# FFN products of 512 columns: the high and the low operand side by side, the RMS factor outside, modulation tiles in other places

## The reference

```python
a = rms_norm(h, norm_ffn[i])
h = h + swiglu(a, ffn_w_gate[i], ffn_w_up[i], ffn_w_down[i])   # (silu(a @ w_gate) * (a @ w_up)) @ w_down, hidden width 2816
```

```python
mod = (jax.nn.silu(c) @ ada_w[i] + ada_b[i])[:, None, :]
mod_c = jax.nn.silu(c_ctx) @ ada_w[i] + ada_b[i]
sh1, sc1, g1, sh2, sc2, g2 = jnp.split(mod, 6, axis=-1)
```

## Time and profile before

| | |
|---|---|
| median of three runs | 2372.78 us (2371.78 to 2374.68) |
| the profiled execution's own time | 2376.23 us |
| its span, first to last instruction | 2374.4 us |
| PE busy | 2285.0 us, 96% |
| VectorE busy | 1706.2 us, 72% |
| ScalarE busy | 1092.3 us, 46% |
| granted TensorE clock, mean | 0.983 |

### The profile page before, as it was taken

How to read it: one execution, slowest core, us unless ns; L and a number is a source line. 1 busy time by engine, 2 the same in 40 slices (tenths; PEclk the granted TensorE clock), 3 DMA queues, 4 the chain that set the end, 5 groups by cost and what they waited for, 6 DMA issues and landing times.

```text
span 2374.4 us, 41274 instructions
## 1 busy us (share of the span) xinstructions
PE 2285.0 (96%) x16984; PEld 2123.7 (89%) x16984; DVE 1706.2 (72%) x3331; ACT 1092.3 (46%) x1968; POOL 0.2 (0%) x4
## 2 busy tenths in 40 slices
PE   7999999999999999999999998999999999998998
PEld 7869999899999999996999986788888888968997
DVE  6678875678777887677787666566877875367667
ACT  4485444564443544447644533544222234275343
POOL 0000000000000000000000000000000000000000
PEclk9899999999999999998999999999999999999999
DMA  6315765347665566641466532022554522423553
GB/s 225 133 46 194 248 210 193 132 154 250 219 203 178 191 242 220 202 173 37 169 242 225 172 107 89 1 72 98 186 166 162 169 89 94 138 81 122 181 180 123
DMA packets 71098, 374.84 MB, mean 158 GB/s; under 512 B 7424, under 2 KB 17664, under 8 KB 38912
## 3 DMA queue, kind: packets, MB, share of 16 engines
q1 hardware_dynamic: 61456, 361.52, 44.6%
q10 hardware_dynamic: 9456, 10.68, 1.5%
HBM read 369.03 MB, written 1.05 MB: 156 GB/s over the span
## 4 chain that ended last, share of the span: by engine, by line
PE 79%; DVE 13%; ACT 4%; DMA 2%; issue 2%; ACTq 0%; DVEq 0%
PE ps L440 74%; DVE w_lo L1558 5%; DMA w_raw<-weights 2%; PE ps L734 2%; ACT w_hi L1042 2%; PE ps L717 2%; DVE ps L1592 1%; DVE hid_f L1927 1%; PE ps L674 1%; DVE a_lo L1558 1%; DVE hid_f L1949 1%; ACT a_hi L1065 1%; PE ps L664 1%; DVE p_ring L2205 0%; DMA X<-x_t 0%
## 5 line engine op out<-in xcount | busy, mean ns | idle before, releaser
L440 PE MATMUL ps<-a_hi,w_hi 128*128 128x256 f32 (+1 forms) x3184 | 941.4, 296 | 39.7 <-DVE w_lo L1558 21.2
L440 PE MATMUL ps<-a_lo,w_hi 128*128 128x256 f32 (+1 forms) x3184 | 932.9, 293 | 0.0
L440 PE MATMUL ps<-a_hi,w_lo 128*128 128x256 f32 (+1 forms) x3184 | 932.6, 293 | 0.0
L1042 ACT CAST w_hi<-w_raw 128x1024 fp32r<-128x1024 f32 (+1 forms) x632 | 593.0, 987 | 499.8 <-DMA w_raw<-weights 498.8
L1558 DVE TENSOR_TENSOR w_lo<-w_raw,w_hi 128x1024 fp32r<-128x1024 f32 (+1 forms) x632 | 699.5, 1148 | 139.6 <-ACT w_hi L1042 139.4
L440 PEld LDWEIGHTS ps<-a_hi,w_hi 128*128 128x128 f32 x3184 | 612.8, 192 | 59.1 <-issue 34.5
L440 PEld LDWEIGHTS ps<-a_lo,w_hi 128*128 128x128 f32 x3184 | 613.0, 193 | 10.7 <-issue 0.2
L440 PEld LDWEIGHTS ps<-a_hi,w_lo 128*128 128x128 f32 x3184 | 612.9, 192 | 10.7
L440 PE MATMUL ps<-hid_hi,w_hi 128*128 128x256 f32 (+1 forms) x1396 | 431.3, 309 | 7.1 <-DVE w_lo L1558 3.1
L440 PE MATMUL ps<-hid_lo,w_hi 128*128 128x256 f32 (+1 forms) x1396 | 427.8, 306 | 0.0
L440 PE MATMUL ps<-hid_hi,w_lo 128*128 128x256 f32 (+1 forms) x1396 | 427.7, 306 | 0.0
(11 more groups left out here) (209 smaller groups left out, 2108.9 us busy)
## 6 DMA issues: line engine op xcount, KB each, us to landing
w_raw<-weights SPq DMA_DIRECT2D x250, 1024.0 KB, 4.8
pe_sb<-weights SPq DMA_DIRECT2D x96, 512.0 KB, 5.6
w_raw<-weights SPq DMA_DIRECT2D x64, 704.0 KB, 4.0
pe_sb<-na_bias ACTq DMA_DIRECT2D x32, 128.0 KB, 2.1
qk<-qk ACTq DMA_DIRECT2D x8, 256.0 KB, 6.9
X<-x_t SPq DMA_DIRECT2D x1, 1024.0 KB, 7.6
X<-c_rows ACTq DMA_DIRECT2D x2, 512.0 KB, 4.5
qk<-ctx_t ACTq DMA_DIRECT2D x1, 1024.0 KB, 5.7
```

The lines of the kernel that those rows point to most:

```text
L440: return nc.tensor.matmul(out, stationary, moving, start=start, stop=stop)
L1042: nc.scalar.copy(w_hi[:, u % SLOTS, c], raw(u, c)).then_inc(hi_split, 1)
```

## The change

Five things are changed together.

1. The high and low operands lie in one tensor (`a_both`, `hid_both`), and in the ffn `wide_tile` makes W_hi [x_hi | x_lo] as one matmul of 512 columns, and adds W_lo x_hi as one of 256 columns into the upper half. The two halves of a PSUM bank are added on the way out: ScalarE copies the upper half (gate and up together, 2 x 256 columns) to SBUF, VectorE adds it to the lower half.
2. The ffn's operand is the unnormalized activation throughout. The gate sum is multiplied with `r_row` before Silu, the up sum isn't, and the output tile of the down part is multiplied with `r_row` before it is added to X. `normalized` goes.
3. Gate and up take the bank pairs (0, 1) and (2, 3) in turn; the first down tile takes bank 0.
4. The order of the splits in gate/up is written out by halves.
5. An ffn has 11 modulation tiles (behind gate/up units 2, 5, 8, ... 20 and behind the down tiles 0, 2, 4, 6); moba gets 4, conv 2, the second nsa 2, the first mlp keeps 36, the last mlp gets 8, with the wait and the sum that finish them.

```diff
-ADA_GATE = [j for j in range(LAZY + 1, FT) if j % 3 != 0]
-ADA_DOWN = range(3)
-ADA_EARLY = 4 * (len(ADA_GATE) + len(ADA_DOWN))
-ADA_MLP = [0, 0, 0, 1, 2, 2, 2, 2] + [1, 1, 1, 1, 2, 2, 2, 2] * 2 + [1, 1, 1] + [0] * 5
+ADA_GATE = range(2, FT, 3)
+ADA_DOWN = range(0, KD, 2)
+ADA_AT = {"ffn": [*ADA_GATE] + [FT + 2 * k + 1 for k in ADA_DOWN], "moba": (1, 3, 5, 7), "conv": (8, 10), "nsa": (0, 2)}
+ADA_EARLY = 4 * len(ADA_AT["ffn"]) + len(ADA_AT["moba"]) + len(ADA_AT["conv"]) + len(ADA_AT["nsa"])
+ADA_MLP = [[0, 0, 0, 1, 2, 2, 2, 2] + [1, 1, 1, 1, 2, 2, 2, 2] * 2 + [1, 1, 1] + [0] * 5,
+           [0, 0, 0, 0, 1, 1, 1, 1] * 2 + [0] * 16]
...
+            def wide_tile(out, high, low, xh, both, start, stop):
+                if not stop:
+                    mm(out, high, both, start, False)
+                last = mm(out[:, S:2 * S], low, xh, False, False)
+                if stop:
+                    last = mm(out, high, both, start, True)
+                return last
...
             def run_ffn(i):                                    # PE
                 operands()
-                a = parts(a_hi, a_lo, CTX)
-                fm_unit("AD", a, between=norm_at)
-                pairs("AD", a, LAZY - 1)
-                operands()
-                pairs("AD", parts(a_hi, a_lo), FT - LAZY)
+                a = wide_parts(CTX)
+                before = cnt.n["D"]
+                wait(pe, taken["A"], cnt.n["A"])
+                for j in range(FT):
+                    if j == 1:
+                        pe.wait_ge(taken["D"], before)
+                    if j >= 2:
+                        pe.wait_ge(taken["A"], cnt.n["A"] - 1)
+                    gate_up(j, a)
...
                 def gate_up(j):                                # ScalarE
+                    gate_sum, at = gate_up_slot[j % 2][:, 0], slice(made[0][0], made[1][0] + 1)
+                    for _, _, (s_, count) in made:
+                        wait(act, s_, count)
+                    wait(act, taken["A"], made[0][1])
+                    nc.scalar.copy(low_slot, ps[:, at, S:2 * S]).then_inc(low_copied, 1)
+                    split_half(u + 2, 0)
+                    act.wait_ge(gate_scaled, h + 1)
+                    nc.scalar.activation(gate_sum, gate_sum, ACT.Silu).then_inc(silu_done, 1)
+                    split_half(u + 2, 1)
                     wait(act, taken["D"], made[1][1] + 1)
                     nc.scalar.copy(hid_hi[:, (h - h0) * S:(h - h0 + 1) * S], t_ring[:, h % 2, 0:S]).then_inc(hid_h, 1)
...
-                def down():                                    # ScalarE
+                def down(k):
                     skip("")
-                    u, [made] = next_unit("D")
+                    u, [made] = unit(cnt, "D", down_banks(k))
+                    bank, p, (s_, count) = made
+                    wait(act, s_, count)
+                    nc.scalar.copy(down_low, ps[:, bank, S:2 * S]).then_inc(low_copied, 1)
                     residual_tile(made, made[1] - d0, gain)
...
                 def gate_up(j):                                # VectorE
+                    both, y = gate_up_slot[j % 2], t_ring[:, h % 2, 0:S]
+                    low_part()                                 # waits for low_copied
+                    v.tensor_tensor(both, ps[:, made[0][0]:made[1][0] + 1, 0:S], low_slot, ALU.add).then_inc(taken["A"], 1)
+                    dve.wait_ge(taken["A"], made[0][1] + 1)
+                    v.tensor_tensor(both[:, 0], both[:, 0], r_row[:, :], ALU.mult).then_inc(gate_scaled, 1)
+                    split_half(u + 2, 0)
+                    dve.wait_ge(silu_done, h + 1)
+                    wait(dve, hid_ready, h - 1)
+                    v.tensor_tensor(y, both[:, 0], both[:, 1], ALU.mult).then_inc(taken["D"], 1)
+                    split_half(u + 2, 1)
                     c = slice((h - h0) * S, (h - h0 + 1) * S)
+                    dve.wait_ge(hid_h, h + 1)
                     minus(hid_lo[:, c], y, hid_hi[:, c]).then_inc(hid_ready, 1)
...
                 def down(k):                                   # VectorE
                     u0, _ = next_unit("")
                     ahead(u0)
-                    u1, [made] = next_unit("D")
+                    u1, [made] = unit(cnt, "D", down_banks(k))
                     bank = ready(made)
-                    x = X[:, k, LAT]
-                    v.tensor_tensor(x, ps[:, bank, 0:S], x, ALU.add).then_inc(taken["D"], 1)
+                    x, total = X[:, k, LAT], down_slot[k % 2]
+                    low_part()
+                    step(v.tensor_tensor(total, ps[:, bank, 0:S], down_low, ALU.add))
+                    sync()
+                    step(v.tensor_tensor(total, total, r_row[:, :], ALU.mult))
+                    sync()
+                    v.tensor_tensor(x, x, total, ALU.add).then_inc(taken["D"], 1)
                     if k < KD - 1:
                         ahead(u1)
...
                     ahead(scaled_unit(lambda m: qk[:, 2 * i + m, 0:S]))   # VectorE, moba
+                    if i in ADA_AT["moba"]:
+                        ada_tile()
...
                     low(2 * i + 1)                             # VectorE, conv
                     ahead(u)
+                    if KD + i in ADA_AT["conv"]:
+                        ada_tile()
```

More of the change, by code:

```diff
@@ L79, in _stream @@
             stage, arg, j = units[u + 1]
-            many = 0
-            if stage == "ffn":
-                many = int(j in ADA_GATE or j in [FT + 2 * k + 1 for k in ADA_DOWN])
-            elif stage == "mlp" and arg == 0:
-                many = ADA_MLP[j]
+            many = int((stage, arg) != ("nsa", 0) and j in ADA_AT.get(stage, ()))
+            if stage == "mlp":
+                many = ADA_MLP[arg][j]
             for _ in range(many):
@@ L236, in raw, with unit @@
             return w_raw[:, u % SLOTS, c]
-        def unit(cnt, rings):
+        def unit(cnt, rings, banks=None):
             u, made = cnt.next("unit"), []
@@ L456, in fm_tile @@
                 weights_at(c)
+                if len(x) == 3:
+                    return wide_tile(out, w_hi[:, slot, c], w_lo[:, slot, c], x[0], x[2], start, stop)
                 xh, xl = x
@@ L520, in parts, with wide_parts @@
                 return [(hi[:, k, cols], lo[:, k, cols]) for k in range(hi.shape[1])]
+            def wide_parts(cols):
+                return [(a_hi[:, k, cols], a_lo[:, k, cols], a_both[:, :, k, cols]) for k in range(KD)]
             def residual_sums():
@@ L890, in down @@
                             pe.wait_ge(hid_ready, n["hid"])
[L891 removed]
+                        xs = [(hid_hi[:, f * S:(f + 1) * S], hid_lo[:, f * S:(f + 1) * S], hid_both[:, :, f * S:(f + 1) * S])
                               for f in range(h * HALF_FT, (h + 1) * HALF_FT)]
[L893 to L896 removed]
+                        fm(ps[:, bank, :], u % SLOTS, 0, xs, h == 0, h == 1).then_inc(unit_done, 1)
+                for k in range(KD):
+                    down(k)
             def run_enter(_):
@@ L1042, in split, with split_half @@
                     nc.scalar.copy(w_hi[:, u % SLOTS, c], raw(u, c)).then_inc(hi_split, 1)
+            def split_half(u, j):
+                if j == 0:
+                    wait(act, landed[u % SLOTS], 16 * (u // SLOTS + 1))
+                c = halves(UNIT_WIDTHS[u])[j]
+                nc.scalar.copy(w_hi[:, u % SLOTS, c], raw(u, c)).then_inc(hi_split, 1)
             def ahead(u):
@@ L1365, in gate_up @@
                 def gate_up(j):
-                    u, made = next_unit("AD")
+                    u, made = unit(cnt, "AD", pair_banks(j))
                     h = cnt.next("hid")
-                    gated = p_ring[:, made[0][1] % 2, 0:S]
-                    if j < LAZY:
-                        act.wait_ge(taken["A"], made[0][1] + 1)
-                        nc.scalar.activation(gated, gated, ACT.Silu).then_inc(silu_done, 1)
-                    else:
-                        wait(act, taken["D"], made[1][1] - 1)
-                        drain(gated, made[0], func=ACT.Silu)
-                    ahead(u)
+                    gate_sum, at = gate_up_slot[j % 2][:, 0], slice(made[0][0], made[1][0] + 1)
[7 more added lines that the diff above has]
+                    split_half(u + 2, 1)
                     wait(act, taken["D"], made[1][1] + 1)
                     nc.scalar.copy(hid_hi[:, (h - h0) * S:(h - h0 + 1) * S], t_ring[:, h % 2, 0:S]).then_inc(hid_h, 1)
-                    if j < 2:
-                        for k in range(4 * j, 4 * j + 4):
-                            high_tile(a_hi[:, k, LAT], norm_slot[k % 2])
                 for j in range(FT):
@@ L1402, in context_tile @@
                     high_tile(a_hi[:, k, CTX], norm_slot[k % 2])
-                for _ in range(KD - 2):
-                    ahead(down())
-                ahead(down())
-                ready_sqrt()
-                u = down()
-                ahead(u)
+                for k in range(KD):
```

(21 more changed lines are left out.)

81 lines of the change are left out of this document (45 added, 36 removed).

## The result

| | before | after |
|---|---|---|
| median of the runs | 2373.11 us | 2399.53 us (2398.58 to 2400.52) |
| ratio, 95% interval | | 1.0111 (1.0094 to 1.0129) |
| span of the profiled execution | 2374.4 us | 2398.7 us |

Slower, as forecast, but by 26.4 us where 16.5 stood. The page of after: the program has 4035 fewer instructions, PE is busy for nearly as long as before, VectorE 74.5 us longer.

What follows compares the result with a forecast made beforehand. TensorE, hardly ever without work in an ffn, was taken as the bound. Gate/up -26.4, down +28.8, ffn ends +9, modulation tiles elsewhere +5 made +16.5 on 2376.2: 2392.7, as a median 2389 us, range 2365 to 2405.

Steps and rivals of the forecast that it cites:

- TensorE's pace: Gate/up: a weight tile takes 0.347 us instead of 0.360, 4.7 us less for an ffn.
- Down: Down stretch: odd split late, TensorE waits 0.8 us, a tile takes 8.52 us instead of 7.92; 28.8 us more in all.
- The rival that hid the narrow matmul's fixed part: Gate/up and down: narrow product's fixed part hides, a tile takes 0.333 us; 2365 us, faster; chance 0.09.
- Gate/up covered: Gate/up: VectorE's late split still arrives 1.2 us before TensorE asks; 1.9 us of waits in units 3 and 4 go.
- End of an ffn: Next stage's first unit: its split comes late, 2.1 us an ffn and 2.75 in the last; 9 us more.
- Modulation tiles elsewhere: Conv 1.7 us for each of two units, moba and last mlp 0.25 some seven times, second nsa nothing; 5 us more.
- Behind the fourth ffn: Stages after the last ffn: 0.7 us more, from the last mlp's modulation tiles; the first mlp keeps its 36.
- VectorE's bound in gate/up: Gate/up: a late VectorE unit takes 5.5 us instead of 4.2; 2445 us, likelier half of this, 2415; chance 0.07.
- a shorter drain chain: Down: the odd split still comes in time, 7.63 us a tile; about 2361 us, faster; chance 0.06.

Runs made afterwards that it cites:

- wide before narrow: Changed kernel with all 512-column matmuls of a product ahead of its 256-column ones, the last wide one at the end: 2398.29 us, ratio 1.0099.
- the narrow down part: Changed kernel with three 256-column matmuls a weight tile in down, without ScalarE's low-half copy and the addition of the halves: 2377.98 us, ratio 1.0010.

## Why the prediction was right in sign and 10 us short

The change lost what the prediction said, where it said. The spans of the profiled executions differ by 24.3 us, 7.8 more than the sum of 16.5 (its terms add up to 16.4). The other 2 us of the 10 lie between these executions and the medians: the one before was 3.1 above its median, as the prediction allowed for, the one after only 1.0. Of the 7.8, TensorE's pace in gate/up makes 7.4 and the three mixers 5.6, of which 4.4 are half clock. Down and the end of the ffns, 2.3 under the forecast, and the part behind the fourth ffn, 3.1 under it, take some of that back, and the latter is luck.

- **TensorE's pace, mis-sized.** The step "a weight tile costs one matmul of 512 and one of 256 columns, 0.347 us" took each width's pace from rows where that width stood alone. In turn they take 0.3525. That is 0.0058 x 336 tiles x 4 = 7.8 us, and gate/up gave 18.2 instead of 25.6. The rival that hid the narrow matmul's fixed part (0.333) erred further the other way. The Trainium skill ("TensorE: Matmul & The Clock Gate", Back-to-back issue gap) gives columns/2.4 + 2.5 ns as the isolated gap of a matmul, which makes an estimate of 0.325 us a tile; this trace does not agree, at 0.3525.
- **Gate/up covered.** Held: no wait for `w_lo`, the waits of units 3 and 4 gone.
- **Down.** Held almost to the number: 8.56 alone (8.52 forecast), 17.93 a pair (17.9), 19.03 in the fourth ffn (1310.89 to 1329.92; 18.9). From T21 to the last down matmul the first ffn took 70.7 us for the forecast 71.2: the pace that was mis-sized in gate/up costs nothing here, where TensorE waits, and its wait at an odd half unit was 0.65 for the forecast 0.8. The mechanism, cover of 0.7 us used up by 1.36 more ahead of the last addition, is shown by three edits that each remove one part: the modulation tile's time, the two links, and the place of ScalarE's cast.
- **End of an ffn.** Held: from the last down matmul to the next RMS row the first ffn took 8.7 us, 6.7 before, and the fourth 9.6, 6.9 before; 2.0 and 2.7 more where 2.1 and 2.75 stood. PE waits 0.92 and 0.52 us in the next stage's first unit where it had lost 0.34. Down and end together were 35.5 for 37.8.
- **Modulation tiles elsewhere.** The step itself nearly held; what it lacked was the clock, and in the second nsa the transfer. Conv's 4.4 us are 2.9 for the two tiles, 1.5 each and not 1.7 (PE waited 1.51 and 2.08, 0.8 in all before), and 1.5 of half clock. Moba's 2.3 are 1.1 of the tiles, which stands at one place, where the chain goes through a weight transfer (5.59 us), the split behind it and a tile, and 1.2 of half clock. In the second nsa the sum had nothing; there it was 1.1 of waiting, which stays when the tiles are made small and goes with their transfers, and 1.7 of half clock. So the tiles cost 5.1 us in the three mixers, for the 4.4 that I had, and the clock 4.4. Whether the tiles' waits bring the clock down is not shown: the executions differ with the same code.
- **Behind the fourth ffn.** The last mlp's tiles cost 0.3, where the step had 0.75. The first mlp ran 1.5 shorter; one piece of its chain took 327.9 us before and 326.4 after, and both numbers come up again in experiments whose code there is the same (327.9 with wide before narrow, 326.4 with the narrow down part), so that isn't the change's.
- **The other rivals.** Neither VectorE's bound in gate/up nor a shorter drain chain was seen.

## What to carry to other kernels

Before an operand is widened to save matmuls, look at what the drain of the product then needs, and who stands behind the drain: here a copy, an addition and a scaling of 0.44 to 0.46 us each in front of one addition, with one more modulation tile in each ffn, cost 35 us over four ffns, and moving one ScalarE cast ahead of work that nobody waited for gave back more than all of it. A pace read where one shape stands alone was too low for shapes in turn (0.347 for 0.3525 us a tile); grouping equal shapes brought some of it back. A small piece of filler work cost over half its time where a drain that was wanted stood behind it (1.5 of 2.67 us in conv) and next to nothing where the product was late (0.3 us for eight in the last mlp): place it by the wait, not by the busy share. Its transfer can cost where its arithmetic does not (second nsa). And before a difference of 1 to 4 us between two profiled executions is put down to an edit, compare the granted clock of the stage in both.
